# Last projection: inverted softmax sums split into a high and a low part and spread for two tiles at once; attention's fills in order of first use

## What is computed

```python
def _fox_prompt_attention(q, k, v, logf):       # per block of 128 queries
    s = jnp.einsum('bqhd,bkhd->bhqk', q_i, k).astype(jnp.float32) * ATTN_SCALE
    s = s + cq_i[..., :, None] - ck[:, :, None, :]
    p = jax.nn.softmax(jnp.where(mask, s, -jnp.inf), axis=-1)
    return jnp.einsum('bhqk,bkhd->bqhd', p.astype(v.dtype), v)
...
att = _fox_prompt_attention(q, k_p, v_p, logf_p)
yp = yp + (att * jax.nn.silu(g)) @ w_out1
```

## Time and profile before

| | us |
|---|---|
| median of 3 runs | 3012.89 |
| lowest and highest | 3012.77, 3015.67 |
| the profiled execution | 3016.5 |
| its span, first to last instruction | 3014.8 |
| outside the span | 1.7 |
| TensorE busy in the span | 2782.4 (92%) |
| VectorE, ScalarE, GpSimd busy | 1601.2, 1028.5, 1391.2 |
| attention, from its first transfer to the next stage's | 1753.5 to 2776.3 |
| `out1`, to the end | 2776.3 to 3014.8 |

### The profile page before, as it was taken

The page is one execution under the profiler, slowest core; times in us unless marked ns, Lnnn a source line. Parts: engine busy times, 40 slices in busy tenths (PEclk is TensorE's granted clock), DMA queues, the critical chain, the costliest instruction groups (busy, mean ns, idle before and its releaser), DMA issues. The chain is left out here.

```text
span 3014.8 us, 46120 instructions
## 1 busy us (share of the span) xinstructions
PE 2782.4 (92%) x17133; PEld 2219.0 (74%) x17133; DVE 1601.2 (53%) x2154; ACT 1028.5 (34%) x1727; POOL 1391.2 (46%) x1012
## 2 busy tenths in 40 slices
PE   6999999598889999999899649999999999998999
PEld 5999999476659999999899635555555555554887
DVE  6233343434546789865555465545545555553432
ACT  6233432323442222211112115445444454444100
POOL 2000000000015874488999637777777777775000
PEclk7999999799989999999999869999999999998999
DMA  4111111165546998887888668787797887874541
GB/s 153 36 36 36 37 37 43 61 200 167 155 138 208 298 294 261 260 277 249 263 258 266 200 144 249 206 243 208 213 247 221 231 227 208 238 215 140 162 123 61
DMA packets 323384, 547.71 MB, mean 182 GB/s; under 512 B 72149, under 2 KB 215673, under 8 KB 314680
## 3 DMA queue, kind: packets, MB, share of 16 engines
q1 hardware_dynamic: 241096, 453.44, 51.1%
q10 hardware_dynamic: 78080, 75.65, 7.6%
q0 software_dynamic: 3984, 15.68, 1.4%
HBM read 449.58 MB, written 95.12 MB: 181 GB/s over the span
## 5 line engine op out<-in xcount | busy, mean ns | idle before, releaser
L1003 POOL TENSOR_TENSOR p_kq<-p_kq 128x1024 f32<-128x1024 f32 x256 | 622.0, 2457 | 384.5 <-DMA p_kq<-in_cache_k_dram 384.0
L1866 POOL TENSOR_TENSOR at_acc<-at_acc,at_w 128x512 f32<-128x512 f32 (+3 forms) x576 | 645.7, 1121 | 228.4 <-ACT at_w L1994 163.9
L95 PE MATMUL p_pb<-p_w,x_xh 128*128 128x256 f32 x2048 | 591.4, 289 | 20.0 <-DVE p_w L1334 20.0
L2029 DVE TENSOR_REDUCE at_mx<-at_mx 128x1 f32<-128x512 f32 (+3 forms) x640 | 382.4, 608 | 426.3 <-PE at_mx L1901 310.8
L96 PE MATMUL p_pb<-p_w,x_xh 128*128 128x256 f32 x2048 | 579.3, 283 | 0.0
L97 PE MATMUL p_pb<-p_w,x_xl 128*128 128x256 f32 x2048 | 578.9, 283 | 0.0
L1994 ACT ACTIVATE at_w<-at_st,c_nckt 128x512 f32<-128x512 f32 (+3 forms) x640 | 390.0, 623 | 366.0 <-PE at_st L1927 189.6
L1436 DVE TENSOR_REDUCE p_sc<-p_kq 128x16 f32<-128x1024 f32 x256 | 309.6, 1216 | 203.2 <-POOL p_kq L1003 202.9
L95 PEld LDWEIGHTS p_pb<-p_w,x_xh 128*128 128x128 f32 x2048 | 390.3, 191 | 32.0 <-DVE p_w L1334 21.5
L96 PEld LDWEIGHTS p_pb<-p_w,x_xh 128*128 128x128 f32 x2048 | 391.8, 191 | 0.0
L97 PEld LDWEIGHTS p_pb<-p_w,x_xl 128*128 128x128 f32 x2048 | 391.4, 191 | 0.0
(11 more groups left out here) (311 smaller groups left out, 3824.5 us busy)
## 6 DMA issues: line engine op xcount, KB each, us to landing
p_kq<-in_cache_k_dram SPq DMA_DIRECT2D x256, 512.0 KB, 4.8
at_vp<-in_cache_v_dram SPq DMA_DIRECT2D x256, 512.0 KB, 5.3
o_mt<-mixed SPq DMA_DIRECT2D x32, 512.0 KB, 5.1
p_raw<-in_w_in_dram ACTq DMA_DIRECT2D x32, 512.0 KB, 5.9
at_q<-qh SPq DMA_DIRECT2D x32, 512.0 KB, 10.9
at_k<-kh SPq DMA_DIRECT2D x32, 512.0 KB, 8.1
c_raw<-in_w_in_dram SPq DMA_DIRECT2D x20, 512.0 KB
mixed<-l_w POOLq DMA_DIRECT2D x8, 1028.0 KB, 4.2
```

The costliest lines, as they stand in the source:

```text
L95: nc.tensor.matmul(out, lhs[0], rhs[0], start=(k == 0), stop=False)
L1003: nc.gpsimd.tensor_tensor(kq[:, slot[page]], kq[:, slot[page]], kq[:, slot[query]], ALU.mult).then_inc(kmul, 1)
L1866: nc.gpsimd.tensor_tensor(t[:, 512 - wd:512], t[:, 512 - wd:512], W[n % RW][:, 0:wd], ALU.add).then_inc(accd, 1)
L2029: nc.vector.reduce_max(mx[:, u % 2, j, seg:seg + 1], MX[r % 2][:, 0:wd], AX.X).then_inc(mread, 1)
```

## The change

In `out1`, the inverted sums now go back into `ls`; ScalarE copies 256 columns of them (two tiles, a pair of `PAIRS`) rounded into rows 0 to 15 of `rl` (`sums_hi`), VectorE writes what the rounding lost into rows 32 to 47 (`sums_lo`), and rows 16 to 31 are zeros from one fill by GpSimd. `expand` has the 0/1 matrix twice, in the same rows, and is made by ScalarE with two copies out of the identity. `spread_out` then does one rounded (float32r) product per block of features for both tiles: 48 rows, 256 columns, 8 products for a pair instead of 16 full ones. There are nine pairs; the last has the 8 sample tokens alone. TensorE does `spread_out` of the next pair ahead of the product of each odd tile.

In `attention`, the fills go in the order in which they are used: GpSimd makes the causal mask first, then the upper rows of `Q2[0]` (all 64 rows of ones; before, zeros and one row of ones), VectorE fills `KM[0]` and `K2[0]` and rounds the mask, ScalarE rounds the identity. VectorE's fills of `KM[1]` and `K2[1]` stand behind MN of unit 0 and of unit 1. `headmask`'s eight selections are steps HM of the schedule, at QK steps 5, 11, ... 47. The waits on `made` go to the steps that use what was filled.

```diff
+        for x in range(8):
+            side.setdefault(5 + 6 * x, []).append(("HM", x))
...
                 if x == 2 and h < 2:
-                    sp.wait_ge(padd, 3 * h + 2)
+                    sp.wait_ge(padd, 2 * h + 1)
...
         def _(pool):
+            nc.gpsimd.memset(maskf[:], 0.0).then_inc(masked, 1)
...
+            nc.gpsimd.memset(Q2[0][HD:P].bitcast(F32), 1.0).then_inc(onesd, 1)
...
+            pool.wait_ge(padd, 2)
+            nc.gpsimd.memset(K2[0][HD:HR].bitcast(F32), 1.0).then_inc(made, 1)
...
+            pool.wait_ge(padd, 4)
+            nc.gpsimd.memset(K2[1][HD:HR].bitcast(F32), 1.0).then_inc(made, 1)
...
+                elif w[0] == "HM":
+                    base, mult = ((0, 1), (HD - 1, -1))[w[1] // 4]
+                    hm = headmask[32 * (w[1] % 4):32 * (w[1] % 4) + 32, :]
+                    pool.wait_ge(hmd, w[1] + 1)
+                    pool.wait_ge(accd, added)
+                    nc.gpsimd.affine_select(out=hm, in_=hm, compare_op=ALU.is_ge, fill=0.0, base=base,
...
-            pe.wait_ge(made, 6)
-            pe.wait_ge(dvm, 2)
+            pe.wait_ge(dvm, 1)
+            pe.wait_ge(idm, 1)
...
+            nc.scalar.activation(identr[:], C.ident[:], ACT.Copy).then_inc(idm, 1)
...
-            for s in range(2):
-                for t in (Q2, KM, K2):
-                    nc.vector.memset(t[s][HD:P].bitcast(F32), 0.0).then_inc(padd, 1)
-            dve.wait_ge(masked, 3)
+            nc.vector.memset(KM[0][HD:P].bitcast(F32), 0.0).then_inc(padd, 1)
+            nc.vector.memset(K2[0][HD:P].bitcast(F32), 0.0).then_inc(padd, 1)
+            dve.wait_ge(masked, 2)
             nc.vector.tensor_copy(maskr[:], maskf[:]).then_inc(dvm, 1)
-            nc.vector.tensor_copy(identr[:], C.ident[:]).then_inc(dvm, 1)
...
+                    if u < 2:
+                        nc.vector.memset((KM, K2)[u][1][HD:P].bitcast(F32), 0.0).then_inc(padd, 1)
```

and in `out1`:

```diff
+    LOW = 32
+    HL = LOW + z.H
+    PAIRS = [(m, 2 * P * m, min(2 * P, z.TS - 2 * P * m)) for m in range((N + 1) // 2)]
...
+            def sums_hi(m, col, width):
+                act.wait_ge(recd, min(2 * m + 2, N))
+                nc.scalar.activation(rl[0:z.H, ds(col, width)], ls[:, ds(col, width)], ACT.Copy).then_inc(r_hi, 1)
...
+            def sums_lo(m, col, width):
+                dve.wait_ge(r_hi, m + 1)
+                nc.vector.tensor_tensor(rl[LOW:HL, ds(col, width)], ls[:, ds(col, width)], rl[0:z.H, ds(col, width)].bitcast(F32),
+                                        ALU.subtract).then_inc(r_lo, 1)
...
-            def turn_out(n, rows, col):
-                pe.wait_ge(recd, n + 1)
-                if n >= 2:
-                    pe.wait_ge(divided, n - 1)
+            def spread_out(m, col, width):
+                pe.wait_ge(r_lo, m + 1)
+                if m:
+                    pe.wait_ge(divided, 2 * m)
                 for k in range(z.KB):
-                    last = nc.tensor.matmul(rb[:, n % 2, k, 0:rows], expand[:, k * P:(k + 1) * P], rl[:, ds(col, rows)],
-                                            start=True, stop=True)
+                    last = nc.tensor.matmul(rb[:, k, 0:width], expand[:, k * P:(k + 1) * P], rl[:, ds(col, width)], start=True, stop=True)
                 last.then_inc(spread, 1)
...
             for n, rows, col in TILES:
-                if n + 1 < N:
-                    turn_out(*TILES[n + 1])
+                if n % 2 and n // 2 + 1 < len(PAIRS):
+                    spread_out(*PAIRS[n // 2 + 1])
                 product(n, rows)
```

More of the change, by code:

```diff
@@ L1841, in _ @@
             nc.gpsimd.memset(onesh[:], 1.0).then_inc(made, 1)
-            pool.wait_ge(made, 6)
-            for base, mult, off in ((0, 1, 0), (HD - 1, -1, 0)):
-                for x in range(4):
-                    pool.wait_ge(masked, (3 if mult == 1 else 7) + x)
-                    hm = headmask[32 * x:32 * x + 32, :]
-                    nc.gpsimd.affine_select(out=hm, in_=hm, compare_op=ALU.is_ge, fill=0.0, base=base,
-                                            pattern=[[mult, z.D]], channel_multiplier=-mult * HD).then_inc(masked, 1)
@@ L2170, in mixed_hi @@
                 nc.scalar.activation(mh[:, n % 2, :, 0:rows], md[:, n % 2, :, 0:rows], ACT.Copy).then_inc(m_hi, 1)
+            def sums_hi(m, col, width):
+                act.wait_ge(recd, min(2 * m + 2, N))
+                nc.scalar.activation(rl[0:z.H, ds(col, width)], ls[:, ds(col, width)], ACT.Copy).then_inc(r_hi, 1)
+            for x, n in ((0, LOW), (LOW, z.H)):
+                nc.scalar.activation(expand[x:x + n].rearrange("p (h d) -> p h d", d=z.HD),
+                                     C.ident[0:n, 0:z.H].rearrange("p (h o) -> p h o", o=1).broadcast_to([n, z.H, z.HD]), ACT.Copy).then_inc(exd, 1)
+            act.wait_ge(rzero, 1)
+            sums_hi(*PAIRS[0])
             m = 0
@@ L2211, in _ @@
             invert(*TILES[1])
+            sums_lo(*PAIRS[0])
             divide(0, P)
@@ L2222, in _ @@
             for n, rows, col in TILES:
-                if n + 2 < N:
-                    invert(*TILES[n + 2])
+                pair = n // 2 + 1 if n % 2 == 0 and n + 2 < N else None
+                if pair:
+                    for tile in TILES[n + 2:n + 4]:
+                        invert(*tile)
                 if n + 1 < N:
                     divide(n + 1, TILES[n + 1][1])
+                if pair:
+                    sums_lo(*PAIRS[pair])
+                if n + 1 < N:
                     mixed_lo(n + 1, TILES[n + 1][1])
```

64 lines of the change are left out of this document (34 added, 30 removed).

## The result

| | before | after |
|---|---|---|
| median of 4 runs on one chip, us | 3013.85 | 2981.61 |
| lowest and highest | 3012.77, 3015.67 | 2976.59, 2985.84 |
| ratio, 95% interval | | 0.989, 0.9878 to 0.9901 |
| profiled execution, its span | 3016.5, 3014.8 | 2985.84, 2984.1 |
| attention, from its first transfer to the next stage's | 1022.8 | 1014.25 |

The change makes the kernel 1.1% faster. The prediction said 2976.7 us, range 2971 to 2988.5, and the median lies in it. It forecast 36.2 us off; by the medians it is 32.2 (29.8 to 36.8 by the interval). On another chip the same kernel gave 2976.83 us (2974.94 to 2978.41, 4 runs) against 3011.95 of before, 35.1 off. The profiled execution is the slowest of the first four, which lie 9 us apart; what the profiles show of such differences comes with the experiments.

The account below looks back on a forecast made before the run. TensorE was taken as the bound, with avoidable work in `out1`'s spreads and waiting at attention's start. 25.0 us from `out1` and 11.2 from attention, 36.2 off the median 3012.89, gave 2976.7 us, range 2971 to 2988.5.

Parts of the forecast that it names:

- The new one, 1.14 us: In `out1`, one spread of 8 rounded 256-column products: 8 x 0.118 + 0.2 = 1.14 us; seven cost 8.0.
- The bounds for 48 rows, 0.113 to 0.246: In `out1`, limits on us per start of a rounded 256-column product with 48 rows, which no row showed; 0.118 taken.
- Rival (b): In `out1`, rounded 48-row products go at 0.246 us a start: 7.2 us less gain, 2983.9 us; chance 0.07.
- The narrow spread, 0.9, and the clock, 1.6: End of `out1`: half the records for 8 sample tokens save 0.9 us; the clock's fall behind them goes, saving 1.6.
- The head of `out1`, 0: Start of `out1`: 1.8 us of added chain against 1.7 saved in the first spread; booked 0, from -1 to +1.
- The chain of a pair, 6.7 us under a cover of 10.9: In `out1`'s loop, VectorE's work for a pair takes 6.7 us, hidden by a product of 10.9 us.
- Rival (d): In `out1`, VectorE's and ScalarE's chain for a pair comes on the path: slower than before, over 3012.9 us; chance 0.02.
- First M 12.0 us earlier, by the loads: Attention's start: loads set the first M at 1761.2, 12.0 us earlier than 1773.25; bounds 1759.9 to 1763.5.
- The rounding of the mask: Attention's start: VectorE's rounding may end only with a GpSimd fill, about 1759.6 or 1761.5; first M not before 1759.6.
- First QK 11.7 us earlier: Attention's start: first QK at 1773.4, just as loads land, with 0.3 us lost to the `KM[1]` fill; 11.7 us gained.
- `headmask`, 0.5 lost: Attention's first 48 steps: eight selections of 1.09 us between GpSimd's sums lose 0.5 us, 0 to 3.
- Rival (a): In attention, late loads or pages, or the shared port, give back the head start: 11.2 us, 2987.9; chance 0.13, full or half.

Follow-up runs that it names:

- the extra load: The kernel after with one more 512 KB transfer, to a tile not in use, ahead of attention's first three loads: 2982.74 us (2 runs).

## Why the prediction was right

- **What bounds it.** Right. The lead at attention's start, 10.5 us once the first head runs, reaches the end of the stage whole, and all of the spread was on the path.
- **The old spread, 2.18 us.** Right, 2.20 by the period.
- **The new one, 1.14 us.** Too small: 1.35 by the same reading, 1.41 by the period. The pace of 0.118 held: inside the block the records start 0.12 us apart. The step that failed is the 0.2 for the way in and out, which was taken as what the old block's 1.97 us leave of 2.18. But inside the old block the records start 0.112 us apart, 16 of them are 1.79, and the way in and out was 0.39. Part of it, the long first and last record (0.21 and 0.20), lay inside the 1.97 and was priced as pace, where halving the records seemed to halve it. The new block has the same 0.39. This cost 1.5 us over seven blocks: 30.8 - 9.9 = 20.9 and not 22.5.
- **The bounds for 48 rows, 0.113 to 0.246.** The number of rows didn't matter: 0.12 with 48 where the earlier trace rows have 0.118 with 128, and at full precision 0.112 with 16 and with 48. Rival (b) is out.
- **The narrow spread, 0.9, and the clock, 1.6.** Together 3.7 - 1.2 = 2.5, right. The reason for the second, that half of the narrow stretch is gone, is not borne out: the same block at full precision had no fall either. So the 1.6 us came true for a cause that stays open.
- **The head of `out1`, 0.** First product at 12.59 us behind the stage's start (12.53 before), first division at 7.84 (7.78). Right, while its first products lost 0.2 more to the clock.
- **The chain of a pair, 6.7 us under a cover of 10.9.** It took 6.3 (2830.26 to 2836.58 in one pair), and no spread behind the first waited. Rival (d) is out. `out1` in all: 20.9 + 2.5 - 0.2 = 23.2; predicted 25.0.
- **First M 12.0 us earlier, by the loads.** In the profiled execution 11.3; in the others it came at 7.6 to 8.0 us behind the first transfer, so 11.8 to 12.1 earlier. Right in size and in mechanism, which the extra load shows against the profile's own releaser.
- **The rounding of the mask.** The prediction let it end with one of GpSimd's fills. It was issued 0.09 us ahead of the fill and took 0.23; before it was issued 0.08 behind one and took 0.97. The Trainium skill, SBUF — State Buffer, section Who interferes with whom, says that where VectorE works in a mode with two ports, as a cast can, whoever issues first gets the shared pair for the whole instruction. The trace agrees in both rows; the mode itself stands in none. So 1759.6 was no bound here: the mask was ready at 1759.16, and the cast had come first.
- **First QK 11.7 us earlier.** 10.1 to 10.8. The fill of `KM[1]` cost 0.75, not 0.3: it started 0.48 us late and 1.76 don't fit into the 1.53 of idle time. The last load landed 20.4 to 21.5 us behind the first transfer and not 19.7, although it was issued at 4.98 and not at 7.12. Both limits came out near 21.
- **`headmask`, 0.5 lost.** Nothing lost: the lead is 10.5 us at the end of the first head and 10.5 at the eighth. It grows by 0.3 in the ninth head and by 0.3 behind the last, to 11.1; what brings these 0.6 is not shown.
- **Attention in all, 11.2.** Measured free of falls, 11.2. That the sum is met so closely is luck: first QK gained 1 us less than forecast, and the 0.5 that weren't lost with the 0.6 that nobody forecast make up for it. The profiled execution shows 8.6, since 1.5 went to the clock and 0.9 to a late store. Rival (a) is out: head 1's M didn't wait, and no lead was given back at the places that it names.

The profiled executions differ by 30.7 and not 36.2: 1.0 in stages that weren't touched, 2.6 in attention (1.5 of it clock and 0.9 the late store), 1.9 in `out1`. Falls of the clock inside attention are not in the prediction's text at all. By what belongs to the kernel the gain is 23.2 + 11.2 = 34.4 us; the medians gave 32.2 on one chip and 35.1 on another.

## What to carry to other kernels

Price a short block of products by its records times the larger of a floor (0.112 us here) and the time of the columns, and add the way in and out apart (0.4 us here): a mean over many records hides it. When a start has several lanes, ask for each when it lands before one of them is shortened. Compare a stage between executions head by head, and read the granted clock there, before a difference of a few microseconds is explained: two differences of 1.5 and 0.9 us looked alike, and only one was the clock.

## What the runs showed of the hardware

- The granted clock drops for some 3 us inside attention, none to two times an execution, 1.5 us each. All fourteen falls stand at the same steps of an odd head, at one or the other of its repetitions, with the same instructions and waits as where none came. They are up to 3 of the 9 us between runs of one kernel; 4.6 of the 7.5 us between the two profiled executions of the kernel after lie ahead of attention.
- Rounded products with 48 rows, TensorE busy 9.3 of 9.7 us, left the granted clock at 0.50; it rose 5.4 us after the first 128-row product, where it had been 4.8 without them.
- Full precision at 256 columns takes 0.216 us a record and rounded 0.118: the doubled number of records and the nearly doubled time of each make 3.64 us against 1.14. Without the change of type the wider block saves 0.5 us against two narrow ones (3.88 against 4.40), and the clock then took more than that.
- A profile's releaser can be an instruction that merely ended last: twice in this case a load had set the start.
